# Four heads of the sample group's attention, each in its own 32 columns of the matmul array

## The reference, cut to what matters

```
s_past = einsum('bqhd,bkhd->bhqk', q, k_past) * scale          # 8 sub-heads
s_new  = einsum('bqhd,bkhd->bhqk', q, k) * scale               # causal among the 4 new tokens
p = softmax(concat([s_past, s_new]));  a = p[:, :, 0] - lam * p[:, :, 1]      # per head
out = einsum('bhqk,bkhe->bqhe', a[..., :p_len], v_past) + einsum(..., a[..., p_len:], v)
```

## Time and profile before

| | us |
|---|---|
| median of 3 runs | 1546.99 |
| lowest, highest | 1539.96, 1550.16 |
| span of the profiled execution (the page gives no other time of it) | 1539.1 |
| sample group's attention in it, from 648.5 to 854.7 us | 206.2 |

### The profile page before, as it was taken

One profiled execution on the slowest core, in us unless ns is written; L12 is line 12 of the kernel. 1 busy time (PEld: TensorE's weight loads), 2 busy tenths in 40 slices (PEclk: granted clock), 3 DMA queues, 4 the chain that ended last, 5 costly groups with the idle time before them and its releaser, 6 DMA issues.

```text
span 1539.1 us, 20098 instructions
## 1 busy us (share of the span) xinstructions
PE 1306.9 (85%) x5769; PEld 883.9 (57%) x5770; DVE 744.7 (48%) x1101; ACT 568.3 (37%) x786; POOL 283.7 (18%) x289
## 2 busy tenths in 40 slices
PE   4879999999997799789999899638989989899920
PEld 1334444366665466566565688426767777677720
DVE  4863232201113887511011454567865556888747
ACT  4530111000001556422232122206755546777633
POOL 0020000010000111000000011112554344554424
PEclk9989999999998999999999899758999999999965
DMA  8981200011100200077664311406875765888545
GB/s 288 367 318 32 82 28 26 16 46 42 41 0 0 84 1 1 1 233 237 193 173 126 127 41 42 183 16 247 303 269 200 272 251 218 313 303 324 216 157 184
DMA packets 84544, 230.86 MB, mean 150 GB/s; under 512 B 16101, under 2 KB 28517, under 8 KB 72165
## 3 DMA queue, kind: packets, MB, share of 16 engines
q1 hardware_dynamic: 70288, 203.80, 37.6%
q0 software_dynamic: 14192, 26.24, 4.8%
HBM read 220.42 MB, written 34.21 MB: 165 GB/s over the span
## 4 chain that ended last, share of the span: by engine, by line
PE 64%; DVE 10%; DMA 9%; issue 7%; ACT 5%; POOL 2%; DVEq 2%; ACTq 1%; SPq 1%; POOLq 0%
PE psum L530 19%; PE psum L583 12%; PE psum L611 11%; PE psum L690 4%; DMA xg<-h_scratch,gidx 4%; PE psum L517 4%; PE psum L705 2%; PE psum L629 2%; DMA wada<-in_w_ada_dram 2%; PE psum L638 2%; DVE xgL L1493 1%; ACT pexp L922 1%; DVEq L332 1%; PE psum L672 1%; DMA wgu<-in_w_up_dram 1%
## 5 line engine op out<-in xcount | busy, mean ns | idle before, releaser
L583 PE MATMUL psum<-wqkv,hT 128*128 128x512 f32 (+1 forms) x432 | 187.5, 594 | 0.0
L611 PE MATMUL psum<-hT,wcv 128*128 128x352 f32 x576 | 170.9, 459 | 0.0
L1485 DVE TENSOR_TENSOR wguL<-wgu,wguH 128x2048 fp32r<-128x2048 f32 x64 | 146.7, 2294 | 39.9 <-ACT wguH L1034 39.2
L530 PE MATMUL psum<-wguH,xgH 128*128 128x512 f32 x320 | 130.8, 409 | 33.0 <-DVE xgL L1493 33.0
L611 PEld LDWEIGHTS psum<-hT,wcv 128*128 128x128 f32 x576 | 109.3, 190 | 60.6
L583 PEld LDWEIGHTS psum<-wqkv,hT 128*128 128x128 f32 (+1 forms) x432 | 77.8, 182 | 103.2 <-issue 103.1
L1034 ACT CAST wguH<-wgu 128x2048 fp32r<-128x2048 f32 x64 | 120.3, 1912 | 23.5 <-issue 14.2
L530 PE MATMUL psum<-wguH,xgL 128*128 128x512 f32 x320 | 126.7, 396 | 0.0
L530 PE MATMUL psum<-wguL,xgH 128*128 128x512 f32 x320 | 126.4, 395 | 0.0
L1553 POOL TENSOR_SCALAR small<-small 128x1 f32<-128x1 f32 (+3 forms) x36 | 20.1, 559 | 508.4 <-ACT ajunk L1011 213.5
L629 PE MATMUL psum<-kT,qz 128*128 128x512 f32 (+3 forms) x192 | 77.7, 520 | 19.5 <-ACT pexp L922 18.2
(11 more groups left out here) (269 smaller groups left out, 2412.1 us busy)
## 6 DMA issues: line engine op xcount, KB each, us to landing
wgu<-in_w_gate_dram SPq DMA_DIRECT2D x32, 1024.0 KB, 4.9
wgu<-in_w_up_dram SPq DMA_DIRECT2D x32, 1024.0 KB, 7.5
wdn<-in_w_down_dram SPq DMA_DIRECT2D x32, 1024.0 KB, 7.4
wada<-in_w_ada_dram SPq DMA_DIRECT2D x24, 1024.0 KB, 8.2
kseq<-in_cache_k_dram SPq DMA_DIRECT2D x64, 256.0 KB, 3.0
vseq<-in_cache_v_dram SPq DMA_DIRECT2D x64, 256.0 KB
yg<-y_scratch SPq DMA_DIRECT2D x16, 512.0 KB, 4.9
wqkv<-in_w_in_dram SPq DMA_DIRECT2D x1, 6144.0 KB, 25.3
```

Source lines behind the costliest of these rows:

```text
L530: ins = mm(out, r32(x(c)), r32(w(c)), start=(begin and c == 0 and k == 0), stop=(end and c == chunks - 1 and k == 2))
L583: last = mm(psum[0:n, 2 + j, :], hT[:, c, P * t:P * t + n], wqkv[:, c, AW * j:AW * j + AW], start=(c == 0), stop=(c == DC - 1))
L611: last = mm(psum[:, 3 * (n % 2) + j, 0:TB], wcv[i % 2][:, c, j, :], hT[:, c, TB * tb:TB * tb + TB], start=(c == 0), stop=(c == DC - 1))
L1485: TT(r32(wguL[slot][:, g, :, :]), wgu[slot][:, g, :, :], wguH[slot][:, g, :, :], ALU.subtract).then_inc(S["wguL_done"], 1)
```

## The change

Each head's queries sit in columns 0 to 7 of its own 32, and each head's scores go to its own 32 partitions of PSUM, 32h to 32h + 31, which is the group of 32 array columns at 32h. The four matmuls of a page no longer add up. The value products become one matmul per head and page: 32 stationary columns, 128 streamed columns, again into the head's own 32 partitions. VectorE and ScalarE then work on 128 partitions in place of 32, with rows that hold no query masked by the constants `pair`, `sub0` and `sub1`. Order and number of all other instructions are the same.

```diff
@@ page_scores
-            for c in range(4):
-                last = nc.tensor.matmul(psum[0:32, 2 * (s % 2) + p // 4, P * (p % 4):P * (p % 4) + P], qbd[:, s, c, :], kTp[n % 2][:, c, :],
-                                        start=(c == 0), stop=(c == 3))
+            for c in range(HEADS):
+                last = nc.tensor.matmul(psum[CG * c:CG * c + CG, 2 * (s % 2) + p // 4, P * (p % 4):P * (p % 4) + P],
+                                        qbd[:, s, c, :], kTp[n % 2][:, c, :], start=True, stop=True)
@@ sample_values
                 for p in range(PAGES + 1):
-                    if p < PAGES:
-                        last = mm(psum[:, 6, :], aTs[s % 2][:, p, :], vseq[s % 2][:, p, :], start=(s == 0 and p == 0), stop=False)
-                    else:
-                        last = mm(psum[:, 6, :], aTs[s % 2][0:LNEW, p, :], vnew[s % 2][:, :], start=False, stop=(s == NSEQ - 1))
+                    m, src = (P, vseq[s % 2][:, p, :]) if p < PAGES else (LNEW, vnew[s % 2][:, :])
+                    for h in range(HEADS):
+                        last = mm(psum[CG * h:CG * h + CG, 6, 0:P], aTs[s % 2][0:m, p, CG * h:CG * h + CG], src[:, P * h:P * h + P],
+                                  start=(s == 0 and p == 0), stop=(s == NSEQ - 1 and p == PAGES))
@@ new tokens' scores
-                for c in range(4):
-                    last = mm(psum[0:32, 7, 256:256 + LNEW], qbd[:, s, c, :], kTs[:, c, LNEW * s:LNEW * s + LNEW], start=(c == 0), stop=(c == 3))
+                for c in range(HEADS):
+                    last = mm(psum[CG * c:CG * c + CG, 7, 256:256 + LNEW], qbd[:, s, c, :], kTs[:, c, LNEW * s:LNEW * s + LNEW], start=True, stop=True)
@@ scalar engine
-                A(pdec[b][:, 0:PAGES * P], psum[0:32, 2 * b:2 * b + 2, :].rearrange("p b n -> p (b n)"), ACT.Exp, bias=m,
+                A(pdec[b][:, 0:PAGES * P], psum[:, 2 * b:2 * b + 2, :].rearrange("p b n -> p (b n)"), ACT.Exp, bias=m,
...
-                nc.scalar.copy(orow[:, h, :], psum[32 * h:32 * h + 32, 6, P * h:P * h + P]).then_inc(S["oT_sb"], 1)
+                nc.scalar.copy(orow[:, h, :], psum[CG * h:CG * h + CG, 6, 0:P]).then_inc(S["oT_sb"], 1)
@@ vector engine
-                            a = 8 * c + 4 * u
+                            a = LNEW * u
...
-                RED(dmx[:, 0:1], psum[0:32, 2 * b:2 * b + 2, :].rearrange("p b n -> p (b n)"), AX_X, ALU.max)
+                RED(dmx[:, 0:1], psum[:, 2 * b:2 * b + 2, :].rearrange("p b n -> p (b n)"), AX_X, ALU.max)
```

More of the change, by code:

```diff
@@ L30 @@
 PAGES = 8
+CG = 32
 NG, EPG = 4, 8
@@ L83, in constants @@
     put("valid", ok.astype(np.float32))
-    r = np.arange(SUBS * LNEW)
+    r = np.arange(P)
     put("dmask", np.where(np.arange(LNEW)[None, :] <= (r % LNEW)[:, None], 0.0, NEG).astype(np.float32))
     cols = np.arange(HEADS * LNEW)
-    put("pair", ((r // (2 * LNEW))[:, None] * LNEW + (r % LNEW)[:, None] == cols[None, :]).astype(np.float32))
-    put("sub0", ((r // LNEW) % 2 == 0).astype(np.float32)[:, None])
-    put("sub1", ((r // LNEW) % 2 == 1).astype(np.float32)[:, None])
+    used = r % CG < 2 * LNEW
+    put("pair", (used[:, None] & ((r // CG)[:, None] * LNEW + (r % LNEW)[:, None] == cols[None, :])).astype(np.float32))
+    put("sub0", (used & (r % CG < LNEW)).astype(np.float32)[:, None])
+    put("sub1", (used & (r % CG >= LNEW)).astype(np.float32)[:, None])
     put("tilecol", i[:, None].astype(np.float32))
@@ L195, in build @@
         kTp = [at(f"kTp{i}", O_H + 24 * K + 2 * K * i, [P, 4, P]) for i in range(2)]
-        pdec = [at(f"pdec{i}", O_H + 4 * K * i + 512 * i, [32, PAGES * P + LNEW]) for i in range(2)]
+        pdec = [at(f"pdec{i}", O_H + 4 * K * i + 512 * i, [P, PAGES * P + LNEW]) for i in range(2)]
         aTs = [at(f"aTs{i}", O_H + 9 * K + 5 * K * i, [P, PAGES + 1, P]) for i in range(2)]
-        snew = [at(f"snew{i}", O_H + 19 * K + 64 * i, [32, LNEW]) for i in range(2)]
-        pairs = [at(f"pairs{i}", O_H + 19 * K + 128 + 64 * i, [32, 16]) for i in range(2)]
+        snew = [at(f"snew{i}", O_H + 19 * K + 64 * i, [P, LNEW]) for i in range(2)]
+        pairs = [at(f"pairs{i}", O_H + 19 * K + 128 + 64 * i, [P, 16]) for i in range(2)]
         orow = at("orow", O_X + 32 * K, [NSAMP, HEADS, P])
@@ L260, in build @@
         lsum = small[:, 48:52]
-        dmx, dl, dr = small[0:32, 52:57], small[0:32, 57:60], small[0:32, 60:64]
-        sgn = small[0:32, 64:65]
+        dmx, dl, dr = small[:, 52:57], small[:, 57:60], small[:, 60:64]
+        sgn = small[:, 64:65]
         ss2, rs2 = small[:, 66:75], small[:, 75:84]
@@ L1138, in _ @@
             dve.wait_ge(W["const_in"], 16)
-            link(STT(sgn, C("sub1", 32), neglam[0:32, :], C("sub0", 32), ALU.mult, ALU.add))
+            link(STT(sgn, C("sub1"), neglam, C("sub0"), ALU.mult, ALU.add))
             for b in range(ADAB):
@@ L1288, in sample_maxima @@
                 dve.wait_ge(W["ds_ps"], s + 1)
-                TT(snew[b][:, :], psum[0:32, 7, 256:256 + LNEW], C("dmask", 32), ALU.add).then_inc(S["dnew_done"], 1)
+                TT(snew[b][:, :], psum[:, 7, 256:256 + LNEW], C("dmask"), ALU.add).then_inc(S["dnew_done"], 1)
                 dve.wait_ge(W["dnew_done"], s + 1)
-                RED(dmx[:, 0:1], psum[0:32, 2 * b:2 * b + 2, :].rearrange("p b n -> p (b n)"), AX_X, ALU.max)
+                RED(dmx[:, 0:1], psum[:, 2 * b:2 * b + 2, :].rearrange("p b n -> p (b n)"), AX_X, ALU.max)
                 link(RED(dmx[:, 1:2], snew[b][:, :], AX_X, ALU.max))
@@ L1311, in sample_pairs @@
                 link(TT(dr[:, 1:2], dr[:, 0:1], sgn, ALU.mult))
-                TS(pairs[s % 2][:, :], C("pair", 32), dr[:, 1:2], None, ALU.mult).then_inc(S["pair_done"], 1)
+                TS(pairs[s % 2][:, :], C("pair"), dr[:, 1:2], None, ALU.mult).then_inc(S["pair_done"], 1)
             dve.wait_ge(W["attT_ps"], 8)
```

## The result

The changed kernel takes **1497.61 us** (median of 4 runs, 1494.28 to 1504.62), the kernel before beside it 1543.47 (4 runs, 1534.02 to 1550.16). The ratio is **0.9696 with a 95% interval of 0.9663 to 0.973**: faster by 3.0%, or 46 us. (The terms that the prediction names for that end, 1504 less 7, give 1497.)

A forecast was written before the change was run, and what follows sets the result against it. TensorE, with 64% of the chain, was taken as the bound. With SP and VectorE followed, the output projection moves from 856.3 to 817.7: -38 us, span 1501, and 1509 from the median 1547.0; range 1498 to 1549.

The forecast's parts named there:

- that end: Low end of the forecast range, stated as 1498: SP at 18.3 us a cycle throughout, 43 us gained, 1504, less run spread 7.
- 7.9 above the span: Last step of the sum: the median of the runs, 1547.0, lies 7.9 above the profiled span, turning 1501 into 1509.
- The step of 0.125 per head: Scores and values on TensorE: each head step takes 0.125 us (0.11 to 0.16), a head's second instruction following its first by 0.11.
- forecast sign of 4 to 5: Sign of being right: the 64 value matmuls with their eight of the new tokens take 4 to 5 us.
- a complete overlap would still give about 817: Even with heads fully overlapped, SP's path puts the output projection at about 817, so at most some 42 us gained.
- No overlap (1545): First rival: the four groups stream one after the other, only values save 0.2 us a sequence, about 1545; chance 0.17.
- A drain for each change of group (1611): Second rival: each of 496 column-group changes costs 0.13 us like a shape change, 64 us, no overlap, 1611; chance 0.13.
- SP is the cover that goes: Sample stage: TensorE's cycle falls to 19.7 us, level with SP's 18.3 to 19.8, so SP's issues must be followed.
- Seven cycles of TensorE: Sign of being right: seven sequence cycles in the sample stage at 19 to 20.5 us, where a cycle took 25.4.
- The long SP row of 759.72: SP's key issue, 15.83 us long because it waits for transposes; without that wait its cycle would be 19.3 us.
- `woutL` is late next: Stage's end: VectorE's eight operations of 9.15 us end after the last value matmul, putting the output projection at 817.7.
- The clock term: Sample stage: half clock costs TensorE 11.4 us over eight value passes, or 1.4 a sequence, called a small term.

The follow-up runs named there:

- values_only: Kernel before with only the value products in the four column groups, scores as before: 1504.49 us, ratio 0.9712.
- router_loads_by_pool: Changed kernel with the five output-projection and router weight loads issued by GpSimd, ahead of the sample stage's loads, not by SP: 1484.97 us, ratio 0.9599.
- two_groups_adjacent: Changed kernel with the value products of heads 0 and 1 in one column group, 2 and 3 in a second, in that order: 1501.61 us (one execution).
- all_moved: Changed kernel with value loads and the five weight loads issued by GpSimd, and five of VectorE's eight `woutL` operations inside the loop: 1464.46 us, ratio 0.9483.

## Why the prediction was right in its way and wrong in its size

The step that failed is the last one of the sum, from the profiled span to the median: the gain of 38 us read in one execution was taken off a median of 1547.0, with "7.9 above the span" carried over to the changed kernel. Of the 11.4 us between 1509 and 1497.61, 3.5 lie in the span (1501 forecast, 1497.5 measured) and 7.9 in this step, for the changed kernel's median lies 0.1 above its profiled span. The points below go from what held to this.

- **The score matmuls of the groups overlap: right, and by more.** The step of 0.125 per head (bounds 0.11 to 0.16), "the second of a head holds back the first of the next", was the wrong picture. All four first instructions start within 0.02 us, then all four second ones. A page's scores take 0.36 us (forecast 0.61, before 0.99), a value pass 2.4 at the full clock (forecast 4.6, before 8.1). That the passes of the changed kernel take 3.6 to 4.2 us, near the forecast sign of 4 to 5, is luck: they run mostly at 1.2 GHz. The larger overlap gave back no time, because SP bounds the stage either way; the prediction's sentence that a complete overlap would still give about 817 was the right one.
- **No overlap (1545): did not occur.** The Trainium skill, TensorE: Matmul & The Clock Gate, Part 3, lets weight loads run under matmuls only when the row groups differ. The traces do not agree: all four groups use all 128 rows, and the second four loads of the page above start at 736.158 to 736.178, under its first four matmuls (736.132 to 736.449). The prediction drew from that rule that the heads would wait for one another, which the page does not say of column groups. The same part says that matmuls start in the program's order without reordering; the adjacent order on two groups, whose pass begins with a pair 13 ns apart, does not agree with that, as far as the order of the compiled instructions can be told.
- **A drain for each change of group (1611): did not occur.** Starts of neighbours in different groups lie 7 ns apart. The Trainium skill, TensorEngine Tiling (Array Packing), Key Properties, says that tiles work independently and that a change of the mode, and not just of the tile, drains; for the tiles the traces agree. Where the shape changes, from the last transpose (735.929) to the first score (736.132), it is 0.20 us where the step is 0.11; whether that is a drain no run shows.
- **SP is the cover that goes: right in the sum, not cycle by cycle.** Seven cycles of TensorE were forecast at 19 to 20.5 us. They took 12.4, 15.0, 33.6, 18.2, 18.9, 17.3 and 20.7: the first holds no value pass (it was 15.6 before, so the prediction should have counted six), the second runs ahead on loads already made, the third waits for keys behind the weight loads, and the last four go at SP's step, 18.7 in the mean. The last keys were forecast for 778.2, 129.7 us after the first transpose; they go 129.0 after it (780.06 - 651.06). The long SP row of 759.72 has no successor. The prediction did not name the five weight loads on SP, but had their time in the row-by-row shift, since their place stays the same in time.
- **`woutL` is late next: right.** Its end was forecast as what holds the output projection, 169.2 us after the stage's start; it starts at 168.1. That the 1.1 us are so few is in part luck. The last pass but one took 4.2 us where 6.0 were put in. The small matmuls of L686 behind it, which were to keep their 2.05, took 3.69 at 1.2 GHz, so that from that pass to `woutL` it was 4.1 and not 2.6.
- **The clock term failed, and with it the step to the median.** The prediction took 1.4 us a sequence as lost before, in the one execution profiled, and treated the stage's gain of 38.6 as what the median would gain. But in the kernel before every microsecond at 1.2 GHz costs TensorE's path about half a microsecond, and how many there are differs from one execution to the next: 26.9 in that profile, 38.5 and 38.6 in two others. In the changed kernel there are 92 and 93, and they cost the stage little, because SP's steps set it up to the last values: the runs with two groups have 62.8 and 57.7 us at 1.2 GHz, and stages of 168.6 and 166.8. Only at the end is TensorE on the chain, with 4.2 and 3.69 us where the full clock's are 2.4 and 2.05. The gain therefore includes most of what the clock had cost before. With 212.6 for the stage of before, and 167.7 for that of the changed kernel, it is 44.9 us, where the sum said 38.6. On the profiled pair the sum was off by 1.1.
- **"7.9 above the span" was no fixed part around the span.** In all executions of the record, time and span differ by 1.7 to 1.9 us (1499.39 and 1497.5; 1545.4 and 1543.5). So the profiled execution took about 1541 and was a quick one among 1539.96 to 1550.16; that it was the one profiled is bad luck, and that the spread was not asked about is the fault. What a usual one has more lies in the sample stage: in the two further profiles the span is 4.4 and 3.9 us longer than 1539.1, and the stage 4.7 and 4.9 longer. The range's low end, 43 us of gain, was taken from SP's steps alone and left this out; the 5 us of clock more at that end would have held the time, as would the 1497 that its own terms give.
- **What stays open.** Why the time at 1.2 GHz differs between executions of one program no run shows. On 1547 the ratio is a gain of 47 us; 44.9 is the stage. The remaining 2 us are less than the part behind the stage varies between profiles of one kernel (677.6 and 680.3 us in the two further profiles of the kernel before).

## What to carry to other kernels

Where a change takes an engine off the critical path, its worth is not what the engine saves but the distance to the next bound, and that must be followed issue by issue; here the second engine's steps of 18 to 20 us stood in the rows of before and gave the stage to 1.1 us. Where the engine that is relieved runs at a clock that varies between executions, the gain carries all of that variation: compare the profiled execution with the spread of the runs first, and set the range by both ends of the clock. And four matmuls with 32 stationary columns each, put in four groups of columns, took TensorE's time down by a factor of 2.8 (a page's scores, 0.99 to 0.36 us) to 3.7 (the 64 value matmuls, 7.17 to 1.96), so look at once for who feeds it.

## What the runs showed of the hardware

- Four column groups, each with all 128 rows, run at the same time: starts 7 ns apart, then, in a pass at the full clock, 0.11 us until each group's next (values_only). Two groups start in pairs in either order of the program.
- In the kernel before the stage has 26.9 to 38.6 us at 1.2 GHz, in the changed kernel 92 and 93, with less work for TensorE and more waits. Neither alone orders the runs: with 29.2 us of waits for DMAs go 93.0 at 1.2 GHz (changed), with 12.5 76.4 (router_loads_by_pool), with 21.4 62.8 (two_groups_adjacent), with 6.1 34.2 (values_only) and with 1.2 44.1 (all_moved). So what lowers the clock here is not shown. Value passes behind the small matmuls of L686 and a wait run at 1.2 GHz: 3.64 us where 1.96 is the full clock's.
- SP's 1.1 us for a page of 256 KB is only to a third the issue itself (0.34 us, L417 and L424); reading the page's number into a register (L408) takes 0.44. Whether reading several numbers at once shortens it was not tried.
